# Two attention maps of a head subtracted ahead of one transpose and one value product, and the last heads' turn moved between output chunks

## What is computed

```python
h = rms_norm(x, attn_norm_g)
a_val, a_gate, p_in, q, k, v = jnp.split(h @ w_in, splits, axis=-1)
y_conv, y_pool = conv_mixer(a_val, a_gate, ...), pool_mixer(p_in, ...)
# diff_attention, per head and query block; m = 0, 1 are the head's two maps
p = jax.nn.softmax(s - slopes * dist, axis=-1)      # causal
a = p[:, :, 0] - lam * p[:, :, 1]
o = a @ v
# after it
o = rms_norm(o, attn_sub_norm_g) * (1 - lam_init)
mix = jnp.concatenate([y_conv, y_pool, y_attn], axis=-1)
x = x + mix @ w_out
x = x + hier_moe(rms_norm(x, ffn_norm_g), ...)
```

## Time and profile before

| | |
|---|---|
| time, median of 3 | 1734.75 us (1733.8 to 1734.77) |
| the profiled execution's own time | 1734.27 us |
| its span in the profile | 1732.3 us |
| TensorE busy | 1710.4 us, 99% |
| VectorE busy | 1166.3 us, 67% |
| ScalarE busy | 858.6 us, 50% |
| mean granted TensorE clock | 0.998 |

### The profile page before, as it was taken

The page is one execution under the profiler, slowest core; times in us unless marked ns, Lnnn a source line. Parts: engine busy times, 40 slices in busy tenths (PEclk is TensorE's granted clock), DMA queues, the critical chain, the costliest instruction groups (busy, mean ns, idle before and its releaser), DMA issues.

```text
span 1732.3 us, 36948 instructions
## 1 busy us (share of the span) xinstructions
PE 1710.4 (99%) x13912; PEld 1649.7 (95%) x13912; DVE 1166.3 (67%) x2048; ACT 858.6 (50%) x1403; POOL 271.7 (16%) x317
## 2 busy tenths in 40 slices
PE   9999999999999999999999999999999999999998
PEld 8999999999999999788999999999999788999998
DVE  7577756767666567665886655766557666787754
ACT  5555444544444455555554444444437455655443
POOL 1030000011000111543420002000112343340001
PEclk9999999999999999999999999999999999999999
DMA  7435555555555554343455555545545343555554
GB/s 270 144 115 186 184 182 184 183 183 183 177 173 170 173 168 146 112 134 108 165 179 177 172 172 171 180 170 176 177 154 179 119 159 99 170 182 185 188 186 134
DMA packets 84903, 288.73 MB, mean 167 GB/s; under 512 B 9152, under 2 KB 16192, under 8 KB 84544
## 3 DMA queue, kind: packets, MB, share of 16 engines
q1 hardware_dynamic: 80448, 283.08, 49.2%
q10 hardware_dynamic: 4352, 4.20, 0.8%
HBM read 285.89 MB, written 1.34 MB: 166 GB/s over the span
## 4 chain that ended last, share of the span: by engine, by line
PE 90%; DVE 5%; ACT 3%; issue 1%; POOL 0%; DMA 0%; ACTq 0%; DVEq 0%; SPq 0%
PE PS L944 27%; PE PS L946 27%; PE PS L945 27%; DVE w_lo L1602 2%; PE PS L1451 1%; PE PS L1417 1%; ACT S_all L818 1%; ACT w_hi L494 1%; PE PS L1455 1%; PE PS L1425 0%; PE PS L1147 0%; DVE PT L2217 0%; DVE x_lo L1607 0%; PE PS L1396 0%; PE PS L1435 0%
## 5 line engine op out<-in xcount | busy, mean ns | idle before, releaser
L1602 DVE TENSOR_TENSOR w_lo<-raw,w_hi 128x1024 fp32r<-128x1024 f32 x522 | 654.3, 1254 | 298.0 <-ACT w_hi L494 288.4
L944 PE MATMUL PS<-x_hi,w_hi 128*128 128x272 f32 (+1 forms) x2832 | 818.0, 289 | 4.2 <-DVE x_lo L1607 1.7
L946 PE MATMUL PS<-x_hi,w_lo 128*128 128x272 f32 (+1 forms) x2832 | 809.3, 286 | 0.0
L945 PE MATMUL PS<-x_lo,w_hi 128*128 128x272 f32 (+1 forms) x2832 | 807.3, 285 | 0.0
L494 ACT ACTIVATE w_hi<-raw 128x1024 fp32r<-128x1024 f32 x522 | 548.0, 1056 | 466.5 <-PE PS L946 464.3
L944 PEld LDWEIGHTS PS<-x_hi,w_hi 128*128 128x128 f32 x2832 | 534.6, 189 | 13.2 <-issue 8.2
L946 PEld LDWEIGHTS PS<-x_hi,w_lo 128*128 128x128 f32 x2832 | 534.9, 189 | 0.0
L945 PEld LDWEIGHTS PS<-x_lo,w_hi 128*128 128x128 f32 x2832 | 534.0, 189 | 0.3
L944 PE MATMUL PS<-a_hi,w_hi 128*128 128x272 f32 (+1 forms) x1280 | 364.8, 285 | 1.3 <-DVE a_lo L2259 1.3
L946 PE MATMUL PS<-a_hi,w_lo 128*128 128x272 f32 (+1 forms) x1280 | 363.7, 284 | 0.0
L945 PE MATMUL PS<-a_lo,w_hi 128*128 128x272 f32 (+1 forms) x1280 | 363.0, 284 | 0.0
(11 more groups left out here) (321 smaller groups left out, 1299.7 us busy)
## 6 DMA issues: line engine op xcount, KB each, us to landing
raw<-stream SPq DMA_DIRECT2D x522, 512.0 KB, 3.3
biasB<-rpbz ACTq DMA_DIRECT2D x16, 256.0 KB, 3.3
G<-b1mats SPq DMA_DIRECT2D x2, 1024.0 KB, 6.8
raw<-stream SPq DMA_DIRECT2D x6, 256.0 KB, 5.9
h<-xT SPq DMA_DIRECT2D x4, 272.0 KB, 4.7
mat<-mats SPq DMA_DIRECT2D x1, 952.0 KB, 5.4
out<-qk SPq DMA_DIRECT2D x3, 256.0 KB, 2.4
v_tok<-u_rows SPq DMA_DIRECT2D x4, 142.0 KB, 3.1
```

The lines of the kernel that those rows point to most:

```text
L944: pe.matmul(ps, hi, rh, start=first, stop=False)
L945: pe.matmul(ps, hi, rl, start=False, stop=False)
L946: return pe.matmul(ps, lo, rh, start=False, stop=last)
L1602: dve.tensor_tensor(w_lo[:, slot, :], raw[:, slot, :], w_hi[:, slot, :].bitcast(F32), ALU.subtract).then_inc(lo_done, 1)
```

## The change

For each of the 4 heads, VectorE now scales and subtracts the two maps right after their exponentials, in SBUF and in place (`mix_probs`). TensorE turns only the difference (three transposes in place of six), ScalarE copies 384 columns in place of 768, and the value product is three matmuls in place of six, whose result in PSUM is already the head's output. `o_square` and the multiply of `o_norms` read it from PSUM. `turn1` and `pv1` of every head stand one slot later on TensorE than before; `pv1(3)` so comes behind `pool_mix`, at c = 20. The pooled blocks use another PSUM bank and no longer wait for the heads. Chunks 22 and 23 first multiply the pooled blocks of both (keys 2, 3), with `o_turn` of heads 2 and 3 between them, and heads 2 and 3 after that.

```diff
             def turn1(hd):
 
-                pe.wait_ge(exp1_done, 4 * (hd + 1))
-                for m in range(2):
-                    b = pair_bank(hd, m)
-                    pe.transpose(PS[:, b, 0:P], B1S(hd, m, 0, P), ident)
-                    pe.transpose(PS[:, b, P:2 * P], B1S(hd, m, 1, P), ident)
-                    mm = pe.transpose(PS[:, b, 2 * P:3 * P], B1S(hd, m, 1, SEQ)[:, P:2 * P], ident)
+                pe.wait_ge(probs1_mixed, 2 * (hd + 1))
+                b = pair_bank(hd, 1)
+                pe.transpose(PS[:, b, 0:P], B1S(hd, 0, 0, P), ident)
+                pe.transpose(PS[:, b, P:2 * P], B1S(hd, 0, 1, P), ident)
+                mm = pe.transpose(PS[:, b, 2 * P:3 * P], B1S(hd, 0, 1, SEQ)[:, P:2 * P], ident)
                 mm.then_inc(turned1_done, 1)
...
-            def denominators(hd):
+            def mix_probs(hd):
 
                 dve.wait_ge(exp1_done, 4 * (hd + 1))
                 step(dve.reciprocal(b1c(hd, 8, 4), b1c(hd, 4, 4)))
                 step(dve.tensor_scalar(b1c(hd, 10, 2), b1c(hd, 10, 2), lam, None, ALU.mult))
-
-            def mix_heads(hd):
-
-                dve.wait_ge(pv1_out, hd + 1)
-                b = pair_bank(hd, 0)
                 for qt in range(2):
-                    step(dve.tensor_scalar(o_part[:, qt * P:(qt + 1) * P], PS[:, b, SEQ + qt * P:SEQ + (qt + 1) * P],
-                                           b1c(hd, 10 + qt), None, ALU.mult))
+                    k = (qt + 1) * P
+                    step(dve.tensor_scalar(B1S(hd, 1, qt, k), B1S(hd, 1, qt, k), b1c(hd, 10 + qt), None, ALU.mult))
                 for qt in range(2):
-                    dve.scalar_tensor_tensor(o_tok[hd % 2][:, qt * P:(qt + 1) * P], PS[:, b, qt * P:(qt + 1) * P], b1c(hd, 8 + qt),
-                                             o_part[:, qt * P:(qt + 1) * P], ALU.mult, ALU.subtract).then_inc(o_mixed, 1)
+                    k = (qt + 1) * P
+                    dve.scalar_tensor_tensor(B1S(hd, 0, qt, k), B1S(hd, 0, qt, k), b1c(hd, 8 + qt), B1S(hd, 1, qt, k),
+                                             ALU.mult, ALU.subtract).then_inc(probs1_mixed, 1)
...
                 if c == 8:
+                    mix_probs(0)
                     logits(1)
-                    denominators(0)
                 if c == 9:
-                    mix_heads(0)
-                    denominators(1)
-                if c == 10:
-                    mix_heads(1)
+                    mix_probs(1)
...
                 if c == 21:
+                    pool_mix_lo()
                     o_norms(1)
-                    pool_mix_lo()
...
+            for j in range(2):
+                pe.wait_ge(lo_done, IN1 + 4 + j + 1)
+                for x in (0, 1):
+                    if j == 0:
+                        mix_ready(KEYS_B[x])
+                for m in range(2):
+                    out1_part(j, m, (0, 1))
+                if j == 0:
+                    o_turn(2)
+                    o_turn(3)
+            for x in (2, 3):
+                mix_ready(KEYS_B[x])
```

More of the change, by code:

```diff
@@ L711, in _ @@
                     conv_mix_hi()
-                    probs1_out(2)
                     exp1(3)
                 if c == 19:
+                    probs1_out(2)
+                if c == 20:
                     probs1_out(3)
-                if c == 20:
                     o_square(2)
-                    o_square(3)
                 if c == 21:
                     pool_mix_hi()
+                    o_square(3)
                 if c == 22:
@@ L1122, in pv1 @@
                 b = pair_bank(hd, 0)
-                for m in range(2):
-                    at = 6 * P * (hd % 2) + 3 * P * m
-                    for qt in range(2):
-                        for kt in range(qt + 1):
-                            o = at + (P * (kt + 1) if qt else 0)
-                            mm = pe.matmul(PS[:, b, m * SEQ + qt * P:m * SEQ + (qt + 1) * P], PT[:, o:o + P],
-                                           v1[:, kt, hd * P:(hd + 1) * P], start=(kt == 0), stop=(kt == qt), skip_group_check=True)
+                for qt in range(2):
+                    for kt in range(qt + 1):
+                        o = P * (kt + 1) if qt else 0
+                        mm = pe.matmul(PS[:, b, qt * P:(qt + 1) * P], probs1(hd)[:, o:o + P],
+                                       v1[:, kt, hd * P:(hd + 1) * P], start=(kt == 0), stop=(kt == qt), skip_group_check=True)
                 mm.then_inc(pv1_out, 1)
@@ L1238, in beside_in @@
                     scores1(3)
+                if c == 18:
                     turn1(2)
-                if c == 18:
+                if c == 19:
                     pv1(2)
                     turn1(3)
-                if c == 19:
-                    pv1(3)
                 if c == 20:
                     pool_mix()
-                if c == 21:
-                    o_turn(2)
-                    o_turn(3)
+                    pv1(3)
             pe.wait_ge(warm_ready, 1)
@@ L1289, in _, with out1_part @@
             pe.wait_ge(router_w_ready, 1)
[L1290 to L1307 removed]
+            def out1_part(j, m, xs):
+                n = IN1 + 4 + j
+                for x in xs:
+                    mm = pe_out1(n, 4 * m + x, 2 * j + m, KEYS_B[x], False, x == 3)
+                if xs[-1] == 3:
+                    if m == 0:
+                        mm.then_inc(out1_even, 1)
+                    else:
+                        mm.then_inc(chunk_used, 1)
+            for j in range(2):
[10 more added lines that the diff above has]
+                mix_ready(KEYS_B[x])
+            for j in range(KD // 2):
+                if j >= 2:
+                    pe.wait_ge(lo_done, IN1 + 4 + j + 1)
+                for m in range(2):
+                    out1_part(j, m, (2, 3) if j < 2 else (0, 1, 2, 3))
+                    if j > 0:
+                        router(2 * j + m - 2)
             def router_end():
```

67 lines of the change are left out of this document (24 added, 43 removed).

## The result

| | before | changed |
|---|---|---|
| median of the timed runs | 1734.67 us (6 runs, 1733.8 to 1734.92) | 1741.15 us (6 runs, 1739.17 to 1743.99) |
| ratio | 1 | 1.0039, 95% interval 1.0027 to 1.0051 |
| profiled execution | 1734.27 us, span 1732.3 | 1741.32 us, span 1739.2 |

The changed kernel is slower by 6.5 us. The forecast was 1735.5 with a range to 1737.7, so it was wrong.

The account below looks back on a forecast made before the run. TensorE, busy 99% of the span, was taken as the bound. Heads 0 and 1 +0.8 and heads 2 and 3 -0.1 take 1734.27 to 1735.0; the median's 0.5 more gives 1735.5 us, range 1733.2 to 1737.7.

Parts of the forecast that it names:

- the 0.9 us at the output chunks: TensorE's waits of 0.69 and 0.19 us in the output projection would go, worth 0.88 us.
- Removed work: Half the transposes and value matmuls go from TensorE, saving about 0.85 us a head, 3.4 for four.
- Mixing 1.9 us: VectorE's scaling and subtracting in SBUF takes 1.9 us a head, between 1.75 and 2.05, and TensorE now waits for it.
- Head 1, wait 2.3 us: TensorE waits 2.3 us at head 1's transposes for VectorE's mixing, in the input projection.
- +0.8: Heads 0 and 1 together end 0.8 us later than before, the saved work given back in head 1's wait.
- Heads 2 and 3: TensorE waits 1.35 us at head 3's transposes, none at head 2; first multiply with head 2 shifts by -0.1 us.
- Rival 2: Clock falls at the new waits, 1.65 us each: one fall 1737.1, 16 in 100; two 1738.8, 6 in 100.
- Rival 3: The one clock fall at 77.9 goes away, -1.65 us, giving 1733.9 us; 12 in 100.

Follow-up runs that it names:

- 11: The kernel of experiment 9 with GpSimd's second pooling tile in three pieces around the mixings of heads 2 and 3: 1733.88 us.
- experiment 2: The kernel before with only the change's output part, attention left as before: 1735.77 us.
- Experiment 1: The changed kernel with VectorE making the convolution's low part ahead of mixing head 2: 1740.62 us.
- 14: The changed kernel with heads 2 and 3 and GpSimd's second tile as in 11, heads 0 and 1 as changed: 1736.71 us.
- experiment 3: The changed kernel with 20 unused matmuls in TensorE's wait ahead of head 1's transposes: 1739.29 us.
- 13: The changed kernel with 20 unused matmuls ahead of head 1's transposes and 26 ahead of the output tiles that wait for the bank: 1738.25 us.
- 6: The changed kernel with convolution's low part before head 2's mixing, GpSimd's second tile after it, head 1's transposes and value product one chunk later: 1738.35 us.
- 10: The kernel before with only heads 0 and 1 changed: head 1's logits before head 0's mixing, transposes and value products one chunk later: 1734.0 us.
- experiment 9: The changed kernel with both head pairs reordered and GpSimd's second pooling tile held until heads 2 and 3 are mixed: 1738.49 us.
- experiment 4: The changed kernel with head 1's transposes and value product, and ScalarE's copy and squares, one slot later: 1738.09 us.

## Why the prediction was wrong, point by point

The median lies 5.65 us above the forecast. Three terms of the sum make it up: the two falls of the clock, which stood in a rival and not in the sum (3.3 to 3.4 us), the wait of heads 2 and 3, forecast at 1.35 us and measured at 3.0 (1.7 us), and the 0.9 us at the output chunks that did not come back. They add up to 5.9 to 6.0.

- **Removed work: right.** 0.85 us a head was counted; the first pair is 1.9 us shorter where nothing waits (11), against 1.7 less the chunk entries. The two waits at the output chunks were not gained (2): the output tiles wait longer, by 1.4 us (2.0 against 0.6), in experiment 2 as in the changed kernel.
- **Mixing 1.9 us, between 1.75 and 2.05: this step failed too.** It is right alone and wrong beside GpSimd. Four operations took what was worked out (0.68 and 0.75 us in place of 0.68 and 0.70). But "what bounds" was read from VectorE's, ScalarE's and TensorE's timelines, and GpSimd's was left out. Before, VectorE combined the heads out of PSUM; the change makes it work in SBUF, in the very stretch in which GpSimd pools. That made 3.4 us of 1.9 at head 2.
- **Head 1, wait 2.3 us: right** (2.6), the 0.3 being one GpSimd operation of 0.73 us at 50.99 beside it. Without the fall the first pair would be 1.1 us longer (2.6 + 0.2 for chunk entries - 1.7), +0.8 was forecast.
- **Heads 2 and 3: this step failed.** The text says "The low part of the convolution (0.88) lies in the wait for ScalarE". It does on VectorE, but output tiles 1 and 5, the last two of chunk 18, need the bank that this operation releases (`misc_free[1]`, when `x == 0`). The wait came one chunk earlier than forecast, 3.0 us in place of 1.35, and head 3's transposes then waited for nothing. As an estimate, half of the 3.0 us is the place behind the mixing and half its stretch: with a mixing of 1.9 us the copy would end 1.5 us earlier. Experiment 1 shows that moving the low part forward alone gains nothing; with the order of head 3 and GpSimd's place repaired as well (14) the 4.4 us are back.
- **Rival 2, the clock falls at the new waits: this is what happened**, with 6 in 100 for two falls. The second fall came behind the wait for the bank, and not at `turn1(3)` as the rival had it. Its price of 1.65 us a fall was right within what the runs tell (1.9 in experiment 3, 1.0 in 13). With the two falls the forecast was 1738.8; the remaining 2.4 us to 1741.2 are about the 1.7 us by which the wait for the bank is longer than the one forecast, and the lost gain of 0.9 at the output, 2.6 together. What was wrong is the chance: the trace had a fall behind a stretch of small matmuls and no long wait at all, so nothing spoke against a fall, and I took the lack of a row as a reason for a low chance. The changed kernel's trace has the rows that were missing: 3.3 us at 1.2 GHz behind each of the two waits.
- **Rival 3**, the fall at 77.9 going away: it stayed in the changed kernel, at 80 to 85. In the profiles of experiments 3 to 6 it is missing, so it comes in some profiles and not in others.

The sum with measured terms, on the profiled executions: removed -3.4, chunk entries +0.4, waits for mixing and bank +2.6 and +3.0, the end of before's waits -0.9, longer waits of the output tiles +1.4 (2.0 against 0.6), the two falls +3.4, the fall at 30 +0.75: 7.25, against 6.9 between the spans. The removed work and the chunk entries are the prediction's own figures, and the first pair of experiments 10 and 11 gave 0.4 us more than they say (1.9 against 1.7 - 0.2), which is about the difference.

The Trainium skill, "SBUF — State Buffer", section "Who interferes with whom", says that a VectorE operation with two SBUF inputs, or in one of the fast modes that a scaling can enter, and a GpSimd operation that reads SBUF exclude each other for a whole instruction. The trace fits it. VectorE's four operations of head 2, taken one by one, are

```profile
98.33 0.55 DVE L1834 TENSOR_SCALAR S_all<-S_all,small 128x128 f32<-128x128 f32 x1
98.92 0.74 DVE L1834 TENSOR_SCALAR S_all<-S_all,small 128x256 f32<-128x256 f32 x1
99.69 0.67 DVE L1837 SCALAR_TENSOR_TENSOR S_all<-S_all,small 128x128 f32<-128x128 f32 x1
100.29 1.01 DVE L1837 SCALAR_TENSOR_TENSOR S_all<-S_all,small 128x256 f32<-128x256 f32 x1
```

They end at 98.88, 99.66, 100.36 and 101.30, each 0.08 to 0.28 us behind the end of one of the four GpSimd rows shown (98.80, 99.52, 100.22 and 101.02). The lock itself is not shown: the GpSimd rows follow each other with 0.07 to 0.08 us between them, less than any of the four operations takes. As an estimate by this rule, 0.6 to 0.7 us (the length of a GpSimd row) for each of four operations gives 2.4 to 2.8 for them in place of 1.4, so 2.9 to 3.3 for the mixing; 3.36 was measured. The prediction did not weigh it.

## What to carry to other kernels

Before work is moved from PSUM into SBUF on VectorE, read GpSimd's timeline of that stretch too, and place the two engines' work one after the other, in pieces if need be: pushed back whole, GpSimd's tile became the late one (experiment 9). Before a step of an engine is pushed back, list everything that it releases, banks too, and not only the data that it makes. And a saving on the bounding engine that turns into one wait of 2.6 us is not neutral: here the clock behind a long wait cost another 1 to 2 us, so that moving the wait's owner one chunk away was worth 3.1 us (experiment 4), more than the 1.7 us of matmuls saved in that pair.

## What was unexpected of the hardware

- A single idle stretch of 2.59 us on TensorE was followed by 3.3 us at 1.2 GHz; with the stretch filled by unused matmuls, the clock stayed at 2.4 GHz (experiment 3). Shorter waits did it at times (1.4 us in experiments 3, 6, 13 and 14), and it does not come in every execution: the profile of experiment 9 has a wait of 3.4 us at 104.6 to 108.0 and no fall behind it, and its eleven runs lie in two groups, five at 1735.9 to 1737.1 us with a granted clock of 0.997 to 0.999, six at 1738.5 to 1739.7 with 0.994 to 0.996.
- Falls also come while TensorE is never idle, behind the matmuls of 2 columns (26.1 to 28.3 us), in some profiles and not in others. In the profile of the changed kernel:

```profile
26.14 1.84 PE L1069 MATMUL PS<-mat,S_all 128*128 128x2 f32 x16
```

with a granted clock of 0.79 from 29 to 30 and 0.50 from 30 to 33; the profile before has the same matmuls and 1.00 there.
- VectorE and GpSimd hold each other up in both directions: scalings and subtractions of 128 and 256 columns took 1.33 and 1.60 us in place of 0.68 and 0.75 beside GpSimd, and GpSimd's additions 1.5 in place of 0.64 beside VectorE's low parts of 1024 columns, of which the first kept its 1.22 and the next two took 1.66 and 1.59 (experiment 9).
